# Start-up of a two-block transformer kernel: order of the first loads, of the first transposes and of the first block of matmuls

## The reference

```python
mod = jnp.einsum('bd,ldm->lbm', jax.nn.silu(c), w_mod) + b_mod[:, None, :]
sh_m, sc_m, g_m, sh_f, sc_f, g_f = [t[:, None, :] for t in jnp.split(mod[i], 6, axis=-1)]
h = x * (1.0 + sc_m) + sh_m
q_sb, k_sb, v_sb, q_dsa, k_dsa, v_dsa, q_ix, k_ix, w_ix = jnp.split(h @ w_in, idx, axis=-1)
# stick-breaking attention on the first three, top-k attention with rope on the rest, then o @ w_out
```

## Time and profile before

| | us |
|---|---|
| median of 3 runs | 1142.4 (1141.84 to 1143.69) |
| the profiled execution's own time | 1144.01 |
| its span, first to last instruction | 1142.7 |
| TensorE busy | 1124.9 (98%) |
| VectorE busy | 842.5 (74%) |
| ScalarE busy | 627.6 (55%) |
| GpSimd busy | 81.1 (7%) |

### The profile page before, as it was taken

The page is one execution under the profiler, slowest core; times in us unless marked ns, Lnnn a source line. Parts: engine busy times, 40 slices in busy tenths (PEclk is TensorE's granted clock), DMA queues, the critical chain, the costliest instruction groups (busy, mean ns, idle before and its releaser), DMA issues.

```text
span 1142.7 us, 24990 instructions
## 1 busy us (share of the span) xinstructions
PE 1124.9 (98%) x10534; PEld 1079.2 (94%) x10534; DVE 842.5 (74%) x1429; ACT 627.6 (55%) x1075; POOL 81.1 (7%) x103
## 2 busy tenths in 40 slices
PE   8999999999999999999999999999999999999998
PEld 6998799999998999999999999999999999999987
DVE  5698879988876888897575589578565677676643
ACT  3467556645435588666444455734645566555542
POOL 3000013000012000111000034100000000000000
PEclk9999999999999999999999999999999999999999
DMA  9977755899997643566655642843345463655540
GB/s 322 381 235 275 245 176 180 301 327 306 313 313 242 202 148 116 182 217 219 219 185 166 212 149 75 259 149 113 109 150 185 148 221 102 213 189 183 197 170 37
DMA packets 194687, 232.22 MB, mean 203 GB/s; under 512 B 4083, under 2 KB 169555, under 8 KB 194576
## 3 DMA queue, kind: packets, MB, share of 16 engines
q1 hardware_dynamic: 193984, 230.32, 60.6%
q0 software_dynamic: 592, 0.31, 0.2%
HBM read 229.56 MB, written 1.05 MB: 202 GB/s over the span
## 4 chain that ended last, share of the span: by engine, by line
PE 91%; DVE 4%; DMA 2%; issue 1%; ACT 1%; POOL 0%; SPq 0%; DVEq 0%
PE ps L154 90%; PE ps L157 2%; DMA XR<-in_x_dram 1%; DVE hL L196 1%; DVE wlo L187 1%; DMA raw<-in_w_in_even_dram 1%; DVE T L187 1%; DMA MW<-in_w_mod_dram 0%; DVE LT L187 0%; DVE T L196 0%; POOL T L187 0%; DVE XA L193 0%; DVE MR L196 0%; DVE ST L199 0%; ACT RD L166 0%
## 5 line engine op out<-in xcount | busy, mean ns | idle before, releaser
L187 DVE TENSOR_TENSOR wlo<-raw,whi 128x1024 fp32r<-128x1024 f32 (+1 forms) x346 | 409.9, 1206 | 162.3 <-ACT whi L166 161.0
L154 PE MATMUL ps<-hH,whi 128*128 128x256 f32 (+3 forms) x1792 | 517.2, 289 | 2.2 <-DVE hL L196 1.9
L154 PE MATMUL ps<-hH,wlo 128*128 128x256 f32 (+3 forms) x1792 | 504.6, 282 | 1.1 <-DVE wlo L187 1.1
L154 PE MATMUL ps<-hL,whi 128*128 128x256 f32 (+3 forms) x1792 | 505.0, 282 | 0.0
L166 ACT ACTIVATE whi<-raw 128x1024 fp32r<-128x1024 f32 (+1 forms) x346 | 349.5, 1033 | 193.3 <-PE ps L154 131.7
L154 PEld LDWEIGHTS ps<-hH,whi 128*128 128x128 f32 x1792 | 337.8, 189 | 8.8 <-issue 4.5
L154 PEld LDWEIGHTS ps<-hH,wlo 128*128 128x128 f32 x1792 | 338.1, 189 | 1.3 <-DVE wlo L187 1.3
L154 PEld LDWEIGHTS ps<-hL,whi 128*128 128x128 f32 x1792 | 338.4, 189 | 0.4
L154 PE MATMUL ps<-uL,whi 128*128 128x256 f32 x352 | 99.2, 282 | 0.0
L154 PE MATMUL ps<-uH,whi 128*128 128x256 f32 x352 | 99.0, 281 | 0.0
L154 PE MATMUL ps<-uH,wlo 128*128 128x256 f32 x352 | 98.4, 280 | 0.0
(11 more groups left out here) (314 smaller groups left out, 1614.4 us busy)
## 6 DMA issues: line engine op xcount, KB each, us to landing
MW<-in_w_mod_dram SPq DMA_DIRECT2D x47, 1024.0 KB, 6.9
raw<-in_w_up_dram SPq DMA_DIRECT2D x44, 1024.0 KB, 5.5
raw<-in_w_in_dram SPq DMA_DIRECT2D x36, 1024.0 KB, 5.0
raw<-in_w_down_dram SPq DMA_DIRECT2D x27, 1024.0 KB, 6.2
raw<-in_w_gate_dram SPq DMA_DIRECT2D x22, 1024.0 KB, 7.3
raw<-in_w_in_odd_dram SPq DMA_DIRECT2D x12, 1024.0 KB, 7.3
raw<-in_w_in_even_dram SPq DMA_DIRECT2D x8, 1024.0 KB, 9.6
raw<-in_w_down_dram SPq DMA_DIRECT2D x8, 768.0 KB, 6.7
```

The source lines that it names most:

```text
L154: return self.queued(self.e.matmul(out, lhsT, rhs, start=start, stop=stop, skip_group_check=True, **kw), length if pos is None else max(le ...
L187: return self.queued(self.e.tensor_tensor(out, a, b, op), 0.07 + cols(out) / self.RATE)
```

## The change

Four things change, all in the first 60 us as the program is written, with consequences for the order of later instructions:

1. **Loads.** c and b_mod are issued by ACT's queue ahead of its table load. SP begins with the identity and then the large loads. The positions go on POOL's queue once m3 has landed, the meta tokens and the 16 row loads once m5 has. The rope angles become a background track that starts when the positions are due.
2. **Bias and transposes.** The bias rows are turned behind m0's products; `keep_clock(5)` goes. Both first modulation columns are finished ahead of the transposes of x. A fourth bank (2) takes the last transposes. Only the first quarter of x is copied by ACT before blocks 0 and 1 of h are modulated, with the split of the narrow weights between; the other three copies follow.
3. **Stage 0.** Both narrow halves come before both wide halves, in the split order and in the matmuls; `keep_clock(4)` becomes `keep_clock(1)`.
4. **Waits for what is now late.** `vectors` waits until the rows are issued, `even` paces on the rope tables after stage 3, and piece m8 waits for the columns of m6.

```diff
@@ plan_weights
-        if s < 3:
+        if 0 < s < 3:
             p.together(*p.even_first[s])
         else:
             p.whole(*p.even_first[s])
@@ begin
-    pos_in = pool.dma(m.PI, D_["positions"].to_broadcast([128, S]), k.into["pos"])
-    k.meta_in = pool.dma(m.MTR, D_["meta_tokens_2"], k.into["meta"])
+    k.rows_in = k.meta_in = k.rope_tables = k.b_mod = None
...
-    for g, r, src in rows_:
-        k.rows_in = pool.dma(RV[r:r + src.shape[0], g, 0:src.shape[1]], src, k.into["rows"])
-    c_in = sp.dma(RV[0:8, 0, :], vec(D_["c"]), k.into["c"])
+    c_in = k.act_dma.dma(RV[0:8, 0, :], vec(D_["c"]), k.into["c"])
     ident_in = sp.dma(m.CST[:, 0:K_TRI], D_["cst"][:, 0:K_TRI], k.into["ident"])
-    bm_in = sp.dma(RV[0:96, 1, :], vec(D_["b_mod"]), k.into["bm"])
+    bm_in = k.act_dma.dma(RV[0:96, 1, :], vec(D_["b_mod"]), k.into["bm"])
...
     keep_clock(k, 3)
+    pace(k, lambda: 0.0 if 0 in k.mod_sums else None)
     bm_turned = pe.wait_ge(*bm_in).tr(m.ps[5][:, 0:96], RV[0:96, 1, :], ident[0:96, 0:96]).inc()
     bm = dve.wait_ge(*bm_turned).copy(m.V[:, 0:96], m.ps[5][:, 0:96]).inc()
-    keep_clock(k, 5)
...
+    def late_loads():
+        while 3 not in k.mod_loaded:
+            yield None
+        yield due(k.mod_loaded[3])
+        pos_in = pool.wait_ge(*k.mod_loaded[3]).dma(m.PI, D_["positions"].to_broadcast([128, S]), k.into["pos"])
+        start(k, rope_tables(pos_in))
+        while 5 not in k.mod_loaded:
+            yield None
+        yield due(k.mod_loaded[5])
+        k.meta_in = pool.wait_ge(*k.mod_loaded[5]).dma(m.MTR, D_["meta_tokens_2"], k.into["meta"])
+        for g, r, src in rows_:
+            rows_in = pool.dma(RV[r:r + src.shape[0], g, 0:src.shape[1]], src, k.into["rows"])
+        k.rows_in = rows_in
...
     pace(k, lambda: due(x_in))
+    pace(k, lambda: 0.0 if MODS[1] in k.mod else None)
...
-    for j2 in range(4):
-        b = (4, 5, 6, 4)[j2]
-        if j2 < 2:
-            pe.wait_ge(*(silu, bm)[j2])
-        elif j2 == 3:
-            fill(k, b)
-        turned = transpose(j2, b)
+    def x_columns(j2, b, turned):
         k.x_cols[2 * j2] = k.x_cols[2 * j2 + 1] = act.wait_ge(*turned).act(m.LT[:, 512 * j2:512 * j2 + 512], m.ps[b], ACT.Copy).inc(k.bank[b])
+
+    fill(k, 2)
+    pe.wait_ge(*silu).wait_ge(*bm)
+    turned = [transpose(j2, b) for j2, b in enumerate((4, 5, 6, 2))]
+    x_columns(0, 4, turned[0])
+    split_high(k)
+    modulated(k, 0, split_low)
+    modulated(k, 1, split_high)
+    for j2, b in ((1, 5), (2, 6), (3, 2)):
+        x_columns(j2, b, turned[j2])
@@ modulation / tensor_mod
+        if n == FIRST_MODS:
+            yield from bank_of(n - 2)
@@ modulated
     hi = act.wait_ge(*x).act(m.hH[:, j, TOK], t, ACT.Copy).inc()
+    if between:
+        between(k)
@@ even
-        if s < 3:
-            multiply(k, jobs, (0, 1), h, 2 * s, TOK, k.h_low, s == 0, False, True)
+        if s == 0:
+            fill_next(k, 0, 1)
+            keep_clock(k, 1)
+            multiply(k, jobs[:4], (0, 1), h, 0, TOK, k.h_low, True, False, True)
+            fill_next(k, *banks[2:])
+            multiply(k, jobs[4:], (0, 1), h, 0, TOK, k.h_low, True, False)
+        elif s < 3:
+            multiply(k, jobs, (0, 1), h, 2 * s, TOK, k.h_low, False, False, True)
...
+    pace(k, lambda: due(k.rope_tables) if k.rope_tables else None)
@@ program
+        k.act_dma = Loader(nc.scalar, None)
```

More of the change, by code:

```diff
@@ L744, in begin @@
     k.b_mod = dve.inc()
-    ang, turns, r = m.ANG
-    inv, sgn = m.CST[:, K_INV:K_INV + 1], m.CST[:, K_SGN:K_SGN + 1]
-    dve.wait_ge(*pos_in).wait_ge(*ident_in).copy(ang, m.PI).settle().ts(ang, ang, inv, ALU.mult)
-    for out, turn_ in ((m.SIN, 0.0), (m.COS, 0.25)):
-        dve.settle().ts(turns, ang, 1.0 / TWO_PI, ALU.mult, turn_, ALU.add)
-        dve.settle().ts(turns, turns, MAGIC, ALU.add).settle().ts(turns, turns, -MAGIC, ALU.add)
-        dve.settle()
-        if out is m.COS:
-            dve.wait_ge(*sine)
-        dve.stt(r, turns, -C1, ang, ALU.mult, ALU.add)
-        dve.settle().stt(r, turns, -C2, r, ALU.mult, ALU.add).settle().stt(r, turns, -C3, r, ALU.mult, ALU.add)
-        dve.settle().ts(r, r, turn_ * TWO_PI, ALU.add, 3.1415925, ALU.min)
-        angle = dve.settle().ts(r, r, -3.1415925, ALU.max).inc()
-        sine = act.wait_ge(*angle).act(out, r, ACT.Sin, scale=sgn if out is m.SIN else 1.0).inc()
@@ L761, in begin @@
-    k.rope_tables = sine
+    def late_loads():
[11 more added lines that the diff above has]
+        k.rows_in = rows_in
@@ new lines, in rope_tables @@
+    def rope_tables(pos_in):
+        ang, turns, r = m.ANG
+        inv, sgn = m.CST[:, K_INV:K_INV + 1], m.CST[:, K_SGN:K_SGN + 1]
+        sine = None
+        yield due(pos_in)
+        dve.wait_ge(*pos_in).wait_ge(*ident_in).copy(ang, m.PI).settle().ts(ang, ang, inv, ALU.mult)
+        for out, turn_ in ((m.SIN, 0.0), (m.COS, 0.25)):
+            yield dve.clock
+            dve.settle().ts(turns, ang, 1.0 / TWO_PI, ALU.mult, turn_, ALU.add)
+            dve.settle().ts(turns, turns, MAGIC, ALU.add).settle().ts(turns, turns, -MAGIC, ALU.add)
+            yield dve.clock
+            dve.settle()
+            if sine:
+                dve.wait_ge(*sine)
+            dve.stt(r, turns, -C1, ang, ALU.mult, ALU.add)
+            yield dve.clock
+            dve.settle().stt(r, turns, -C2, r, ALU.mult, ALU.add).settle().stt(r, turns, -C3, r, ALU.mult, ALU.add)
+            yield dve.clock
+            dve.settle().ts(r, r, turn_ * TWO_PI, ALU.add, 3.1415925, ALU.min)
+            angle = dve.settle().ts(r, r, -3.1415925, ALU.max).inc()
+            yield due(angle)
+            sine = act.wait_ge(*angle).act(out, r, ACT.Sin, scale=sgn if out is m.SIN else 1.0).inc()
+        k.rope_tables = sine
@@ L773, in transpose @@
         return pe.inc()
-    for j2 in range(4):
-        b = (4, 5, 6, 4)[j2]
-        if j2 < 2:
-            pe.wait_ge(*(silu, bm)[j2])
-        elif j2 == 3:
-            fill(k, b)
-        turned = transpose(j2, b)
-        k.x_cols[2 * j2] = k.x_cols[2 * j2 + 1] = act.wait_ge(*turned).act(m.LT[:, 512 * j2:512 * j2 + 512], m.ps[b], ACT.Copy).inc(k.bank[b])
+    def x_columns(j2, b, turned):
+        k.x_cols[2 * j2] = k.x_cols[2 * j2 + 1] = act.wait_ge(*turned).act(m.LT[:, 512 * j2:512 * j2 + 512], m.ps[b], ACT.Copy).inc(k.bank[b])
+    fill(k, 2)
[7 more added lines that the diff above has]
+        x_columns(j2, b, turned[j2])
+    turned = turned[3]
     turn(k)
@@ L805, in begin @@
     k.q = {}
+    start(k, late_loads())
     start(k, centred())
@@ L821, in vectors @@
     p0, p1 = m.ps[b0], m.ps[b1]
+    while k.rows_in is None:
+        yield None
     yield due(k.rows_in, k.meta_in)
@@ L956, in quarter_chunk @@
     yield due(k.mod_sums[n])
+    while k.b_mod is None:
+        yield None
     row = dve.wait_ge(*k.mod_sums[n]).copy(m.MR[:, at:at + 128], ps[:, 0:128]).inc()
@@ L975, in tensor_mod @@
         pe.wait_ge(*k.mod[MODS[n - 1]])
+    if n == FIRST_MODS:
+        pe.wait_ge(*k.mod[MODS[n - 2]])
     for i in range(4):
@@ L1024, in mod_columns, with modulated @@
     return k.m.MOD[:, c0:c0 + n]
-def modulated(k, j):
+def modulated(k, j, between=None):
     act, dve, m = k.act, k.dve, k.m
@@ L1047, in even @@
     widths = (128, 128, 128, 68) + (128,) * 8
-    fill_next(k, *banks)
     y = [None] * 6
     for s in range(4):
-        modulated(k, 2 * s)
-        modulated(k, 2 * s + 1)
-        if s == 0:
-            keep_clock(k, 4)
+        if s > 0:
+            modulated(k, 2 * s)
+            modulated(k, 2 * s + 1)
         jobs = []
```

## The result

The changed kernel takes **1146.5 us** (median of 9 runs, 1143.9 to 1149.2) against 1142.4 (9 runs, 1141.2 to 1145.2) of the kernel before: a ratio of 1.0033 [1.0018, 1.0047]. I had forecast 1139.1. It is 4 us slower instead of 3.3 faster. The profiled execution took 1147.5 us with a span of 1146.2.

What follows compares the result with a forecast made beforehand. TensorE was taken to set the pace from 34.17 us, with the transfer stream full before and until 60 us. Narrow products of stage 3 ending 3.3 us earlier gave 1142.4 - 3.3 = 1139.1 us, range 1136.4 to 1142.0.

Steps and rivals of the forecast that it cites:

- m0, x and m2 earlier: Start of the kernel: earlier issue and held-back small loads bring these forward by 2.5, 2.5 and 2.1 us.
- The rule behind it: Weight stream at the start: small loads share the engines with large ones, so holding them back frees 1.8 us.
- Stage 1 at 29.0: End of stage 0: TensorE enters stage 1 at 29.0 us, 5.2 us earlier than 34.17.
- m6 at 41.7: Stage 2: VectorE's work and the stream each make m6 start at 41.4 to 42.0 us; 41.7 taken.
- Narrow products of stage 3 end at 56.2: End of stage 3's narrow products: 14.5 us after m6, at 56.2 instead of 59.5, 3.3 us earlier.
- the remaining rope work: VectorE, 34 to 56 us: the rest of 6.2 us of rope operations fits into 8.0 free us, costing nothing.
- What is gained by then arrives at the end in full: From 60 us on: TensorE sets the pace, so the 3.3 us gain reaches the end nearly in full.
- The clock: Rival, stages 0 and 1: TensorE starts at 1.2 GHz, costing 4.5 to 7.8 us; up to 1146.0 us; 7%.
- Given back in the attention part: Rival, 60 to 210 us: TensorE's 1.7 us idle time doubles, 1.6 us of gain left, 1140.8 us; 17%.

Runs made afterwards that it cites:

- e3: Changed kernel with positions loaded first and rope angles made at the start, meta tokens and rows still late: 1142.6 us, 1.0005 of the kernel before.
- e5: Changed kernel with positions and rope angles early, plus ScalarE's exponential table load moved ahead of the RD copies: 1145.9 us, 1.0027 of the kernel before.
- e11: Changed kernel with positions and rope angles early, plus the RV transposes held until the first XR block: 1143.4 us, 1.0008 of the kernel before.
- e8: Changed kernel with rows and meta tokens loaded at the start, positions and rope angles still late: 1145.7 us, 1.0025 of the kernel before.
- e13: Changed kernel with the rope angles' range reduction left out (tables not the reference's): 1144.4 us, 1.0014 of the kernel before.
- e12: Changed kernel with all small loads early, but VectorE's rope work as late as in the changed kernel: 1143.8 us, 1.0015 of the kernel before.
- e6: Changed kernel with all small loads at the start and rope angles early: 1141.4 us, 0.9990 of the kernel before.
- e10: Same kernel as e6, measured again with more rounds: 1142.8 us, 0.9996 of the kernel before.
- e14: Kernel before with one edit, c and the bias rows loaded on ScalarE's queue: 1141.7 us, 0.9994 of the kernel before.
- e9: The e6 kernel with stage 0 in the old order, narrow and wide columns together: 1145.1 us, 1.0021 of the kernel before.
- e0: The changed kernel measured a second time, unedited: 1145.5 us, 1.0025 of the kernel before.
- e2: Changed kernel with the RV transposes held until the first XR block is out, as before: 1146.0 us, 1.0032 of the kernel before.
- e17: The e10 kernel with weight splits held to one block less ahead until the rotation is done: 1148.7 us, 1.0054 of the kernel before.
- e7: Changed kernel with stage 0 in the old order, narrow and wide columns together: 1145.7 us, 1.0032 of the kernel before.
- e4: Changed kernel with ScalarE's exponential table load moved ahead of the RD copies: 1148.1 us, 1.0054 of the kernel before.
- e1: Changed kernel with four dummy products in TensorE's wait ahead of the row transposes: 1145.2 us, 1.0024 of the kernel before.

## Why the prediction was wrong

- *m0, x and m2 earlier*: right, and too small: 3.2, 3.2 and 4.2 us instead of 2.5, 2.5 and 2.1. m2 cost stage 0 only 0.36 us of wait. The rule behind it holds: with all small loads in front m0 starts at 8.9 to 9.3, without them at 6.9 to 7.2. Most of that is one load: with the positions alone in front m0 starts at 8.6 to 8.8 (e3, e5, e11), with the 17 others alone at 7.8 (e8). But by the `RD` copy that gain is gone.
- *Stage 1 at 29.0*: it enters its weights of w3 at 30.11, with 0.76 us of wait for their split, as worked out (30.4). *m6 at 41.7*: 41.62, with the wait for `hL` just ahead.
- *Narrow products of stage 3 end at 56.2*: **wrong by 1.5 us** (57.7). I had costed the remaining rope work at nothing, with 8.0 free us of VectorE between 34 and 56 as its cover. The free time was there, but not ahead of `hL`: 1.03 us of wait at 54.59. Another 0.37 us is a wait for the transfer of m8 at 52.48, which I had not counted. With the short angles of e13 the `RD` copy is 0.65 us earlier, and e12 shows the delay without any late load.
- *What is gained by then arrives at the end in full*: **the step that failed**. Its ground was that TensorE is busy 148.3 of 150 us from 60 to 210. That says who is busiest, not that nobody else sets a time there. At 65 to 67 us ScalarE and VectorE hand over the bank, and they were no earlier than before, with two more weight copies ahead of it. Of the 5.7 us that the profile gives back, 1.85 are that wait, 3.4 the clock behind it, and about 0.5 TensorE's new order. e6, e10, e14 and e9 show that the rule itself is true where that wait is absent; the changed kernel, e0, e2 and e17 what it costs where it isn't.
- *The clock*: I looked for it in stages 0 and 1, where it stayed at 1.00, and named 24 us as the limit. It fell at 68 us and cost 3.4 us in this profile. That this rival's 1146.0 us is close to the 1146.5 measured is chance: it had the low level in another place, and no wait at `KS`. I had also written that the trace of the kernel before shows no drop later. It does, at 360 us, beyond the rows that I had read. The Trainium skill, "TensorE: Matmul & The Clock Gate", section "HAM oscillation — how this bites in real kernels", says that idle gaps bring the clock down for the matmuls behind them. This case agrees that a low level, where there is one, stands behind a wait; it does not stand behind every one (none behind 1.68 us in e17 or 1.87 in e14, one behind 0.64 in e12).
- *Given back in the attention part* was the nearest rival, with less than a third of the size (1.7 us against 5.7): I had doubled the idle time behind, and not looked at the one hand-over where it would fall. In e5, e7, e8 and e13 what this rival describes did happen: TensorE's idle time from 73 to 289 us went from 1.2 to between 2.9 and 4.4 us.
- *Late loads as such* are not what costs. e8 has the rows early and is no faster (1145.7 against 1145.5 and 1146.5); e12 has all loads early and still loses.

What stays open: waits, idle time and clock do not add up to all that is given back. What is left is nothing in e12 and the four kernels above it, 0.2 in e13, 0.4 to 0.8 in the changed kernel, e0, e2, e4, e5, e7 and e8, and 1.1 to 1.3 in e3, e11 and e17. It is no wait: TensorE is busy longer for the same number of matmul records, in another order (from the `RD` copy to `uH` 229.6 us in e3 and 228.5 in the kernel before, both at a clock of 1.00). In e1 it is busy 3.1 us longer, of which the dummies are 2.0. Which rows of the new order take the time was not found. Nor was a kernel tried in which ScalarE's two extra copies alone are moved. That they are the cause of the late `KS` is read from the chain of the changed kernel and from the table, where the wait goes with their number; it is not shown by an edit of them alone. Why the scheduling puts two or three copies there when the angles are late was not looked into.

## What to carry to other kernels

An engine that is 98% busy passes a gain on only if each thing it needs next comes earlier too: follow the first buffer or bank that it must be handed behind the change, and ask what stands ahead of the hand-over on the other engines. Work moved off the critical start must find its free time ahead of the next item that the bounding engine waits for; a sum of free time over 20 us does not show that. Where a schedule is built from due times, an earlier engine also draws more work ahead of the others, so the order has to be read again far behind the edit.

## What I had not expected of the hardware

The granted clock fell to 0.50 in the middle of the run behind a wait of 0.64 us (e12) or 1.85, and it did so differently in two executions of one kernel: 3.4 and 1.7 us lost behind the same 1.85 us. Behind the wait of 1.88 us at 360 us it fell in the profile of the kernel before, and not in that of e14, where TensorE has the same list. In the profile with four dummy products in the wait at 65 us it stayed at 1.00 there; one profile does not show that the dummies did that, though the granted clocks of the eight runs point the same way. Narrow columns first gave 2.3 us (e10 against e9), and most of that was a wait of 3.88 us and the low level behind it that they avoid.
